# Seven block products for eight in the gate/up projections of a two-layer encoder trunk

## What is computed

```python
def swiglu(h, w_gate, w_up, w_down):
    return (jax.nn.silu(h @ w_gate) * (h @ w_up)) @ w_down
# per layer: h = rms_norm(x, ffn_norm_w[layer])
#            x = x + swiglu(h, w_ffn_gate[layer], w_ffn_up[layer], w_ffn_down[layer])
# h: 256 x 2048, w_gate and w_up: 2048 x 5632, w_down: 5632 x 2048
```

## Time and profile before

| | |
|---|---|
| median of 3 runs | 2080.72 us (2079.9 to 2081.82) |
| profiled execution, span from the first to the last instruction | 2078.4 us |
| PE busy | 2069.7 us, 9380 matmuls |
| weight loads into PE busy | 1715.3 us |
| DVE busy | 1234.9 us (59%), 1339 instructions |
| ACT busy | 966.6 us (47%), 1082 instructions |
| POOL busy | 162.7 us (8%) |
| read from HBM | 422.82 MB, with what is written 218 GB/s over the span |

### The profile page before, as it was taken

The page is one execution under the profiler, slowest core; times in us unless marked ns, Lnnn a source line. Parts: engine busy times, 40 slices in busy tenths (PEclk is TensorE's granted clock), DMA queues, the critical chain, the costliest instruction groups (busy, mean ns, idle before and its releaser), DMA issues.

```text
span 2078.4 us, 22665 instructions
## 1 busy us (share of the span) xinstructions
PE 2069.7 (100%) x9380; PEld 1715.3 (83%) x9380; DVE 1234.9 (59%) x1339; ACT 966.6 (47%) x1082; POOL 162.7 (8%) x271
## 2 busy tenths in 40 slices
PE   9999999999999999999999999999999999999999
PEld 8878888888888888888888788888888888888887
DVE  7776655555455554556676677665555455554654
ACT  6565554443444434445555455554443444434443
POOL 1010100000001000011111110101000010000000
PEclk9999999999999999999999999999999999999999
DMA  9665776766567655677767877776765667666673
GB/s 332 219 203 190 248 215 217 235 212 201 185 214 233 220 191 193 210 234 251 234 217 228 245 240 225 237 228 219 227 217 189 201 212 232 209 199 191 212 237 130
DMA packets 216422, 453.66 MB, mean 218 GB/s; under 512 B 10544, under 2 KB 10560, under 8 KB 216064
## 3 DMA queue, kind: packets, MB, share of 16 engines
q1 hardware_dynamic: 197600, 392.72, 57.5%
q0 software_dynamic: 18304, 57.37, 10.2%
q10 hardware_dynamic: 416, 2.13, 0.3%
HBM read 422.82 MB, written 29.36 MB: 218 GB/s over the span
## 4 chain that ended last, share of the span: by engine, by line
PE 50%; issue 32%; DMA 14%; POOL 2%; DVE 1%; ACT 0%; POOLq 0%; DVEq 0%
PE acc L1186 16%; PE acc L1187 16%; PE acc L1192 16%; DMA spread<-blocks 8%; DMA blocks<-folded 6%; POOL spread L525 2%; DMA w_blocks<-w_folded 1%; PE turn_zb L1322 0%; DVE w_lo L804 0%; PE turn_zb L1206 0%; PE turn_zb L1278 0%; POOL w_spread L540 0%; PE turn_zb L1245 0%; PE turn_zb L1264 0%; DVE gs L984 0%
## 5 line engine op out<-in xcount | busy, mean ns | idle before, releaser
L596 ACT ACTIVATE w_hi<-raw 128x1024 fp32r<-128x1024 f32 x744 | 786.5, 1059 | 984.4 <-PE acc L1192 979.9
L804 DVE TENSOR_TENSOR w_lo<-raw,w_hi 128x1024 fp32r<-128x1024 f32 x744 | 900.0, 1220 | 567.8 <-ACT w_hi L596 567.0
L1186 PE MATMUL acc<-w_hi,xT_hi 128*128 128x512 f32 x2016 | 786.3, 390 | 0.0
L1187 PE MATMUL acc<-w_hi,xT_lo 128*128 128x512 f32 x2016 | 784.4, 389 | 0.0
L1192 PE MATMUL acc<-w_lo,xT_hi 128*128 128x512 f32 x2016 | 538.8, 389 | 0.0
L1186 PEld LDWEIGHTS acc<-w_hi,xT_hi 128*128 128x128 f32 x2016 | 378.5, 188 | 79.2 <-issue 0.9
L1192 PEld LDWEIGHTS acc<-w_lo,xT_hi 128*128 128x128 f32 x2016 | 378.5, 188 | 78.6
L1187 PEld LDWEIGHTS acc<-w_hi,xT_lo 128*128 128x128 f32 x2016 | 378.6, 188 | 78.0
L1186 PE MATMUL acc<-w_hi,m_hi 128*128 128x512 f32 x956 | 372.3, 389 | 0.0
L1187 PE MATMUL acc<-w_hi,m_lo 128*128 128x512 f32 x956 | 371.9, 389 | 0.0
L1192 PE MATMUL acc<-w_lo,m_hi 128*128 128x512 f32 x956 | 255.5, 389 | 0.0
(11 more groups left out here) (149 smaller groups left out, 542.1 us busy)
## 6 DMA issues: line engine op xcount, KB each, us to landing
raw<-in_w_gate SPq DMA_DIRECT2D x88, 1024.0 KB, 5.2
raw<-in_w_up SPq DMA_DIRECT2D x88, 1024.0 KB, 6.2
raw<-in_w_down SPq DMA_DIRECT2D x88, 1024.0 KB, 5.1
raw<-in_w_qkv SPq DMA_DIRECT2D x48, 1024.0 KB, 6.1
raw<-in_w_out SPq DMA_DIRECT2D x32, 1024.0 KB, 5.6
raw<-in_w_in SPq DMA_DIRECT2D x26, 1024.0 KB, 5.9
blocks<-folded POOLq DMA_DIRECT2D x42, 512.0 KB, 3.9
spread<-blocks POOLq DMA_DIRECT2D x168, 128.0 KB, 6.1
```

The source lines that it names most:

```text
L596: nc.scalar.activation(w_hi[:, h.slot, :, :], raw[:, h.raw_slot, 2 * h.part:2 * h.part + 2, :], ACTF.Copy).then_inc(hi_ready, 1)
L804: nc.vector.tensor_tensor(w_lo[:, h.slot, :, :], raw[:, h.raw_slot, 2 * h.part:2 * h.part + 2, :], f32(w_hi[:, h.slot, :, :]), ALU.subtrac ...
L1186: nc.tensor.matmul(dst, hi[:, h.k0 + k, at], wh, start=h.opens and k == 0, stop=False)
L1187: nc.tensor.matmul(dst, lo[:, h.k0 + k, at], wh, start=False, stop=False)
```

## The change

In an up iteration that isn't the first of its layer, the first four contraction tiles of gate and up are treated together as a 2x2 by 2x2 block product. The blocks of the left matrix are token tile by even or odd contraction tiles (two tiles in each block), those of the right one are even or odd contraction tiles by gate or up. Winograd's form of Strassen's scheme makes seven block products of it: four sums of activation blocks (once per layer), four sums of weight blocks (every iteration, on DVE) and sums of the products (every iteration, on DVE).

The iteration then has 19 halves for 16. Twelve are as before. Seven ("outer" twice, "P", "Q", "R", "W", "corner") have one output tile for each contraction tile, so six matmuls, four with w_hi and two with w_lo. P, Q, R and W round and split a sum of weights instead of raw weights. Products 1, 5, 6 and 7 have a bank each of turn_zb, and the rest is added straight into acc. The order of the units within the iteration changes with it, raw buffers are released after their last reader, and the split of the folded hid into m_hi and m_lo is 10 steps after the fold instead of 8, except in the last iteration of an up phase. Loads from memory are the same in number and size.

The rstd scale moves: gate leaves acc unscaled as acc + corr, Silu applies the scale in two instructions of 512 columns, and up leaves first as acc + corr and then as corr · rstd · hid.

```diff
+LATE_FOLD_LAG = 10
+SEVEN = [("plain", 0, 4), ("plain", 0, 6), ("outer", 0, 0), ("P", -1, 0), ("plain", 1, 4), ("Q", -1, 0), ("plain", 1, 6), ("corner", 1, 0),
+         ("R", -1, 0), ("plain", 0, 8), ("outer", 0, 2), ("W", 0, 0), ("plain", 0, 10), ("plain", 0, 12), ("plain", 0, 14),
+         ("plain", 1, 8), ("plain", 1, 10), ("plain", 1, 12), ("plain", 1, 14)]
+SEVEN_UNITS = [(0, 4), (1, 0), (0, 0), (1, 4), (0, 8), (0, 12), (1, 8), (1, 12)]
+SUM_AT = {2: "P", 4: "Q", 7: "R", 10: "W"}
+SUMMED = 12
...
+        self.seven = ph.name == "up" and not self.paired
...
+        if self.ph.name == "up" and self.i < self.ph.count - 1:
+            return self.fold_at(c) + LATE_FOLD_LAG
...
+        product = {n: turn_zb[:, q * CH:(q + 1) * CH] for q, n in enumerate((1, 5, 6, 7))}
+        FORMS = {"P": (5, 0), "Q": (7, 2), "R": (6, 1)}
...
-                    sp.wait_ge(lo_ready, 2 * (u - RING) + 2)
-                sp.dma_start(raw[:, h.raw_slot, :, :], src).then_inc(raw_landed[h.raw_slot], 16)
+                    sp.wait_ge(lo_ready, UNITS[u - RING][0].release(u - RING) + 1)
+                sp.dma_start(raw[:, u % RING, :, :], src).then_inc(raw_landed[u % RING], 16)
...
+                elif h.kind in SUMS:
+                    act.wait_ge(sum_made, 4 * SEVENS.index(it) + SUMS.index(h.kind) + 1)
...
+            def round_forms(ph):
...
+                act.wait_ge(s_made, layer + 1)
...
+                nc.scalar.activation(s_hi[:, :, :, :].rearrange("p f k t -> p (f k t)"), tsum[:, 1, :, :].rearrange("p k n -> p (k n)"),
+                                     ACTF.Copy).then_inc(s_rounded, 1)
...
+                if it.seven and t == SUMMED:
+                    act.wait_ge(products_done, 2 * (it.base + SUMMED))
+                    nc.scalar.activation(corr[:, 0, :], product[1], ACTF.Copy).then_inc(first_taken, 1)
...
+                        for tt in range(TT):
+                            ins = nc.scalar.activation(hid[:, tt, :], hid[:, tt, :], ACTF.Silu, scale=rstd[:, tt:tt + 1])
...
+                if it.seven and h.s in SUM_AT:
+                    weight_sum(it, SUM_AT[h.s])
                 dve.wait_ge(hi_ready, h.index + 1)
...
+            def weight_sum(it, form):
...
+                first, second = raw[:, up % RING, even, :], raw[:, up % RING, odd, :]
+                if form == "P":
+                    for u in (gate, up):
+                        dve.wait_ge(raw_landed[u % RING], 16 * (u // RING + 1))
+                    out_to, a, b = tsum[:, 0, :, :], raw[:, gate % RING, even, :], first
+                elif form == "Q":
+                    out_to, a, b = tsum[:, 1, :, :], first, second
+                elif form == "R":
+                    dve.wait_ge(sum_made, 4 * n + 1)
+                    out_to, a, b = tsum[:, 0, :, :], tsum[:, 0, :, :], second
+                else:
+                    dve.wait_ge(sum_made, 4 * n + 3)
+                    out_to, a, b = tsum[:, 0, :, :], tsum[:, 0, :, :], raw[:, gate % RING, odd, :]
+                nc.vector.tensor_tensor(out_to, a, b, ALU.add).then_inc(sum_made, 1)
+
+            def make_forms(ph):
...
+                link(nc.vector.tensor_tensor(x, f32(xT_hi[:, 0:UNIT, :]), f32(xT_lo[:, 0:UNIT, :]), ALU.add))
+                nc.vector.tensor_tensor(forms[:, 2], a11, a21, ALU.subtract)
+                link(nc.vector.tensor_tensor(forms[:, 0], a21, a22, ALU.subtract))
+                link(nc.vector.tensor_tensor(forms[:, 1], a11, forms[:, 0], ALU.subtract))
+                nc.vector.tensor_tensor(forms[:, 3], a12, forms[:, 1], ALU.subtract).then_inc(s_made, 1)
...
+            def corrections(it):
+                n = SEVENS.index(it)
+                dve.wait_ge(first_taken, n + 1)
+                link(nc.vector.tensor_tensor(corr[:, 2, :], corr[:, 0, :], product[6], ALU.subtract))
+                link(nc.vector.tensor_tensor(corr[:, 1, :], product[7], corr[:, 2, :], ALU.add))
+                nc.vector.tensor_tensor(corr[:, 2, :], product[5], corr[:, 2, :], ALU.subtract)
+                nc.vector.tensor_tensor(corr[:, 3, :], product[5], corr[:, 1, :], ALU.subtract).then_inc(corr_made, 1)
...
+                elif it.seven:
+                    n = SEVENS.index(it)
+                    dve.wait_ge(corr_made, n + 1)
+                    if c == 0:
+                        for tt in range(TT):
+                            dve.wait_ge(products_done, 2 * it.last_half(0) + tt + 1)
+                            nc.vector.tensor_tensor(hid[:, tt, :], acc[:, it.pair(0), tt, :], corr[:, tt, :], ALU.add).then_inc(acc_read, 1)
+                        return
+                    for tt in range(TT):
+                        dve.wait_ge(products_done, 2 * it.last_half(1) + tt + 1)
+                        nc.vector.tensor_tensor(corr[:, 2 + tt, :], acc[:, it.pair(1), tt, :], corr[:, 2 + tt, :], ALU.add).then_inc(acc_read, 1)
+                    dve.wait_ge(silu_done, ph.up0 + i + 1)
+                    for tt in range(TT):
+                        dve.wait_ge(acc_read, 2 * ph.chunk(i, 1) + tt + 1)
+                        nc.vector.scalar_tensor_tensor(out=hid[:, tt, :], in0=corr[:, 2 + tt, :], scalar=rstd[:, tt:tt + 1],
+                                                       in1=hid[:, tt, :], op0=ALU.mult, op1=ALU.mult).then_inc(hid_made, 1)
...
+            def seventh(it, h, hi, lo):
...
+                pe.wait_ge(hi_ready, h.index + 1)
+                for k, (dst, (sh, sl), start, stop) in enumerate(made):
+                    wh = w_hi[:, h.slot, k, :]
+                    nc.tensor.matmul(dst, sh, wh, start=start, stop=False)
+                    nc.tensor.matmul(dst, sl, wh, start=False, stop=False)
+                pe.wait_ge(lo_ready, h.index + 1)
+                for k, (dst, (sh, sl), start, stop) in enumerate(made):
+                    ins = nc.tensor.matmul(dst, sh, w_lo[:, h.slot, k, :], start=False, stop=stop)
+                ins.then_inc(products_done, 2)
```

More of the change, by code:

```diff
@@ L96, in __init__ @@
                 firsts, lates = [0, 8], [4, 12]
-            units = ([(c, k) for c in range(2) for k in firsts] + [(c, k) for k in lates for c in range(2)] + units[2 * ph.tiles // UNIT:])
-        self.halves = [Half(base + 2 * u + q, 2 * u + q, c, k + 2 * q) for u, (c, k) in enumerate(units) for q in range(2)]
+            self.units = ([(c, k) for c in range(2) for k in firsts] + [(c, k) for k in lates for c in range(2)] + self.units[2 * ph.tiles // UNIT:])
+        steps = [("plain", c, k + 2 * q) for c, k in self.units for q in range(2)]
+        if self.seven:
+            steps, self.units = SEVEN, SEVEN_UNITS
+        self.unit0 = unit0
+        self.halves = [Half(base + s, s, c, k, self.unit_of(0 if c < 0 else c, k), kind) for s, (kind, c, k) in enumerate(steps)]
         for c in range(ph.chunks):
@@ L105, in __init__, with unit_of, release @@
         self.chunk0 = chunk0
+    def unit_of(self, c, k):
+        return self.unit0 + self.units.index((c, k - k % UNIT))
+    def release(self, u):
+        c, k = self.units[u - self.unit0]
+        last = max(h.s for h in self.halves if h.kind in ("plain", "outer", "corner") and h.c == c and h.k0 - h.k0 % UNIT == k)
+        if self.seven and k == 0:
+            last = max(last, max(t for t, form in SUM_AT.items() if form in ("PW" if c == 0 else "PQR")))
+        return self.base + last
     def last_half(self, c):
@@ L161, in make_phases @@
 def make_phases():
-    out, sums, taken = [], [0] * 6, [0, 0]
+    out, sums, taken = [], [0] * 6, [0, 0, 0]
     for n in range(len(PHASES)):
@@ L174 @@
 HALVES = [(it, h) for it in ITERATIONS for h in it.halves]
+UNITS = [(it, u) for it in ITERATIONS for u in range(len(it.units))]
+SEVENS = [it for it in ITERATIONS if it.seven]
 CHUNKS = [(it, c) for it in ITERATIONS for c in range(it.ph.chunks)]
@@ L403, in f32, with source @@
             return ap.bitcast(F32)
+        def source(h):
+            if h.kind in SUMS:
+                return tsum[:, int(h.kind == "Q"), :, :]
+            if h.kind == "corner":
+                return raw[:, h.raw_slot, 1::2, :]
+            return raw[:, h.raw_slot, 2 * h.part:2 * h.part + 2, :]
         def lhs(ph):
@@ L467, in load_x, with unit @@
                 sp.dma_start(xT_raw[:, k0:k1, :], xT[:, k0:k1, :]).then_inc(xt_landed[piece], 16)
[L469 to L472, removed]
+            def unit(it, n):
+                ph, u = it.ph, it.unit0 + n
+                c, k0 = it.units[n]
+                w, col = weights(ph, it.i, c)
+                row = (ph.hidden0 * GRP if ph.name == "down" else 0) + k0
                 src = w.rearrange("(k p) n -> p k n", p=P)[:, row:row + UNIT, col:col + CH]
@@ L1038, in up_work @@
                 ph, i = it.ph, it.i
+                if it.paired and t == 4:
+                    make_forms(ph)
+                if it.paired and t == 5:
+                    split_forms(ph)
+                if it.seven and t == SUMMED:
+                    corrections(it)
```

(30 more changed lines are left out.)

56 lines of the change are left out of this document (41 added, 15 removed).

## The result

The changed kernel takes 2057.0 us (median of four runs, 2056.6 to 2062.7) where the kernel before, run beside it, takes 2080.3 (2078.2 to 2081.8). The ratio is 0.9894, with a 95% interval of 0.9879 to 0.9910. It is 23.3 us faster where the prediction said 27; the measured time lies in its range (2052.4 to 2062.0), 3.3 us above its number and outside the 2052.5 to 2055.5 that it gave a chance of 0.68.

A forecast was written before the change was run, and what follows sets the result against it. PE, always busy, was taken as the bound, at 226.7 ns a matmul. Span 2078.4 - 27.2 (120 matmuls fewer) + 0.2 = 2051.4, plus 2.3 to the median: 2053.7 us; 8-in-10 range 2052.4 to 2062 us.

The forecast's parts named there:

- What bounds it: Whole kernel: PE is always busy, so time is the number of matmuls times 226.7 ns while halves are ready.
- 120 x 0.2267 = 27.2 us: Up iterations: 120 matmuls go over 20 iterations (9380 to 9260), saving at most 27.2 us.
- the seven small halves last 6 x 0.227 = 1.36 us each: New up iterations: each half of six matmuls was priced at the usual matmul pace, 1.36 us.
- Rival 4: Small halves: summed stationary tiles or bank changes cost PE extra; 0.19 us per matmul would give 2080 us; chance 0.02.
- The forecast is wrong if the span falls by less than 20 us: Whole execution: the sign set beforehand for a failed forecast, a span falling by less than 20 us.
- The narrow place: Start of an up iteration: DVE finishes splitting P (half 3) at 7.28 us, wanted at 7.71; 0.4 us in hand.
- Rival 1: DVE at iteration starts: each step costs its whole duration, stalling PE; 7 us given back, 2061 us; chance 0.16.
- The weight sums: DVE in new up iterations: a sum of two SBUF operands costs 1.13 us between starts, like a split.
- rival 3: DVE weight sums: run at half the pace, 2.27 us for 1.13; 34 us of stall, 2088 us; chance 0.03.
- ACT at step 12: ACT taking m_hi at step 12: comes by at 19.8 us, folded hid lands at 18.7 to 20.7; costed at nothing.
- Ends of up phases: End of layer 0's short up phase: hid is ready 1.20 us later, 1.1 in hand; 0.1 to 0.2 us lost.
- From span to time: Last step of the sum: 2.3 us added to the 2051.4 us span to get the median time, 2053.7 us.

The follow-up runs named there:

- e6: Changed kernel with half W's six matmuls done twice, so 192 matmuls again per new up iteration; 2085.6 us in a single run.
- e8: Changed kernel with 160 unused bytes in front of the forms (s_hi, s_lo, the sums of activation blocks); 2052.6 us, ratio 0.9857.
- e9: Changed kernel with the moving tiles w_hi and w_lo moved by 64 bytes, stationary tiles kept in place modulo 512 bytes; 2074.8 us in a single run.
- e10: Changed kernel with the moving tiles w_hi and w_lo moved by 256 bytes, stationary tiles kept in place modulo 512 bytes; 2057.9 us in a single run.
- e4: Changed kernel with the weight sum P made a second time on DVE, into an unused buffer, right before the real one; 2070.0 us, ratio 0.9940.
- e11: Changed kernel with w_hi and w_lo moved by 32 bytes, m by 96 and the sums of activation blocks by 96; 2106.2 us in a single run.
- e12: Changed kernel with 160 unused bytes in front of all buffers behind the small ones, moving the mixers' tiles too; 2051.2 us, ratio 0.9856.

## Why the prediction was right, and where it missed

- **What bounds it.** Right. Time is matmuls times their distance: e6 gave back exactly what 120 matmuls are worth.
- **"120 x 0.2267 = 27.2 us".** The count was right, the price was not. The step that failed is "the seven small halves last 6 x 0.227 = 1.36 us each". Four of them last about 1.39 to 1.41, and drag on into the plain half behind. Read in the iterations, (43.52 - 42.35) x 20, this term of the sum was 23.3 us for 27.2. The cause is where the forms lie: e8 moves them by 160 bytes and has all of it back (42.16). That what counts is their place against the moving tile, modulo 256 bytes, is inferred from e9 and e10. Rival 4 named the sums among the stationary tiles as a possible reason, and I argued it away with halves that follow each other without a gap and banks that alternate: those rows speak only for tiles in their old places. Rival 4's sign, distances above 227 ns with no releaser, is what came, at a seventh of the 1.36 us an iteration that it spoke of, and I had given it 0.02. Neither of its reasons is the cause: e8 has the same sums and the same banks at 226.7.
- **"The forecast is wrong if the span falls by less than 20 us".** By the profiled executions it fell by 17.5 (2078.4 to 2060.9), and the qkv phase, which was 5.7 us longer in the second, accounts for what is lacking to 23.2; the spans of the three other executions lie 23.0 to 23.6 below 2078.4. One span was too thin a sign for a kernel whose qkv phase varies by 8 us.
- **The narrow place.** Right: 0.4 us forecast; 0.49 by the timeline (659.63 for the load at 660.12); 0.45 to 0.54 by e4. That the steps came out within 0.05 us rests on taking the distances between starts, not the durations. Rival 1 did not occur: splits and sums of 1.22 us start 1.13 to 1.14 apart (654.96, 656.10, 657.23), also where a wait stands between them. The prediction set against this the Trainium skill, "VectorE: DVE Perf Modes", section "The DRAIN you can't avoid", by which the next instruction doesn't start before the pipeline is empty. The same section of the Trainium skill adds that an instruction that isn't held starts earlier; the trace agrees with the addition and not with the bare rule.
- **The weight sums.** Right: 1.22 us each, 1.13 to 1.14 to the next start, as priced. Nothing of rival 3 occurred.
- **ACT at step 12.** Right: it came by 19.6 us after the start (671.97, for 19.8 forecast) and did not have to wait.
- **Ends of up phases.** 0.1 to 0.2 us forecast for layer 0's short phase; none came, its down phase lasts 65.28 us, as before.
- **From span to time.** I took 2.3 us, the median less one span. It is 1.8 in every run of this kernel (2056.8 and 2055.0, for instance), and 1.8 to 2.2 in the runs of the kernel before that were made beside the experiments. With 1.8 and 3.9 us more the sum gives 2051.4 + 3.9 + 1.8 = 2057.1.

That the range held the result is luck in part: its upper end was set for rival 1, whose mechanism did not occur. The forecast's own 2052.5 to 2055.5 did not hold it.

## What to carry to other kernels

When PE is the bound and matmuls are taken away, the others' work is judged at the places where an engine can't run ahead, in distances between starts; the average share says nothing there: at 71% DVE had half a microsecond of room, and one operation more, of 1.13 us, cost some 0.6 us in 14 of 20 iterations (e4). A new operand of the matmul should be put at the same distance to the moving operand (modulo 256 bytes here) as those whose pace is known, and the time from one of its weight loads to the next should be read first: the loss shows in no wait and no clock. Where a median moves by less than the spread of a phase that wasn't touched, iterations between two weight loads still tell kernels apart to a hundredth of a microsecond.

## What the runs showed of the hardware that was not expected

The pace of fp32r matmuls of 512 columns at the full clock depends on where its two operands lie in SBUF. Put as the distance between stationary and moving tile modulo 256 bytes, it is 226.7 ns at 0, 228.9 at 192, and 232.6 to 234.9 at the six other multiples of 32 (table above). A bad place for all operands costs this kernel 2.7%: e11, with all three kinds off, took 2106.2 us, and e12, with all three in place, 2051.2. The Trainium skill, "TensorE: Matmul & The Clock Gate", section "Part 2: What happens when you issue a matmul", says that loading the next tile's weights takes no read bandwidth from the running matmul. The traces do not agree that the two are independent: 64 bytes between them made the matmuls of a down phase 2.2 ns longer in the mean. Through what they meet, and whether it is bandwidth, no run shows. Nor does one show what the 13 ns are by which 226.7 is above 512 columns at 2.4 GHz, 213.3 ns.
